# Order of fill pieces, turning waits and output copies in the attention stage of a one-core hybrid block

## The reference, cut to what matters

```python
z = jnp.einsum('bhqd,bhkd->bhqk', qb, kb) * scale
log_keep = jnp.where(valid, jax.nn.log_sigmoid(-z), 0.0)
later = lax.cumsum(log_keep, axis=3, reverse=True) - log_keep
w = jnp.where(valid, jnp.exp(jax.nn.log_sigmoid(z) + later), 0.0)
outs.append(jnp.einsum('bhqk,bhkd->bhqd', w, vb))
```

## Time and profile before

| what | us |
|---|---|
| three runs | 1004.69, 1006.06, 1008.02 (median 1006.06) |
| the profiled execution | 1006.47 |
| span of the profiled execution | 1004.6 |
| PE busy in the span | 960.1 (96%) |
| DVE, ACT, POOL busy in the span | 526.6, 321.1, 193.8 |
| attention stage, 195 to 347 us | 152.0, of it PE busy 138.65, DVE 111.48, ACT 102.50 |
| from the barrier on, 347 us to the end | 657.6 |

### The profile page before, as it was taken

The page is one execution under the profiler, slowest core; times in us unless marked ns, Lnnn a source line. Parts: engine busy times, 40 slices in busy tenths (PEclk is TensorE's granted clock), DMA queues, the critical chain, the costliest instruction groups (busy, mean ns, idle before and its releaser), DMA issues.

```text
span 1004.6 us, 14136 instructions
## 1 busy us (share of the span) xinstructions
PE 960.1 (96%) x5731; PEld 805.3 (80%) x5731; DVE 526.6 (52%) x763; ACT 321.1 (32%) x732; POOL 193.8 (19%) x96
## 2 busy tenths in 40 slices
PE   4999999899999899999999999999999989999998
PEld 3889999677777688888787788888888778788886
DVE  3676895689668254454224338033334466654422
ACT  6552111467776431211451111123322552110000
POOL 0001120160001022112211212100011016873000
PEclk9799999999999999999999999999999999999999
DMA  9860600611210211211222253511212674436231
GB/s 320 225 177 23 189 2 22 202 49 29 59 43 17 58 43 44 62 42 42 63 74 95 95 126 124 140 43 56 61 54 65 237 243 168 129 123 210 86 103 63
DMA packets 120587, 100.58 MB, mean 100 GB/s; under 512 B 18023, under 2 KB 100544, under 8 KB 120266
## 3 DMA queue, kind: packets, MB, share of 16 engines
q1 hardware_dynamic: 90218, 76.07, 25.0%
q10 hardware_dynamic: 30304, 23.60, 7.9%
HBM read 73.44 MB, written 24.12 MB: 97 GB/s over the span
## 4 chain that ended last, share of the span: by engine, by line
PE 90%; DVE 4%; ACT 2%; issue 2%; DMA 1%; SPq 0%; POOL 0%; ACTq 0%; DVEq 0%
PE psum L758 47%; PE psum L266 8%; PE psum L267 7%; PE psum L268 7%; PE psum L1000 3%; PE psum L985 2%; DVE stick L1095 2%; PE psum L971 2%; PE psum L1322 1%; PE psum L973 1%; PE psum L381 1%; PE psum L370 1%; PE psum L1416 1%; PE psum L1422 1%; PE psum L1398 1%
## 5 line engine op out<-in xcount | busy, mean ns | idle before, releaser
L758 PE MATMUL psum<-hhi,w3hl 128*128 128x512 f32 x1120 | 370.8, 401 | 5.4 <-issue 2.7
L758 PEld LDWEIGHTS psum<-hhi,w3hl 128*128 128x128 f32 x1120 | 211.9, 189 | 51.5 <-issue 6.0
L758 PE MATMUL psum<-hlo,w3hl 128*128 128x512 f32 x560 | 219.4, 392 | 0.0
L747 POOL TENSOR_TENSOR w3hl<-w3raw,w3hl 128x1024 fp32r<-128x1024 f32 x43 | 104.7, 2434 | 514.9 <-DVE w3hl L740 514.9
L758 PEld LDWEIGHTS psum<-hlo,w3hl 128*128 128x128 f32 x560 | 106.0, 189 | 21.8 <-issue 1.9
L1095 DVE TENSOR_TENSOR_SCAN stick<-stick,floor 128x1024 f32<-128x1024 f32 (+7 forms) x64 | 94.3, 1511 | 25.4 <-ACT stick L1045 25.3
L266 PE MATMUL psum<-w1hi,hhi 128*128 128x256 f32 (+2 forms) x320 | 99.2, 310 | 0.0
L267 PE MATMUL psum<-w1lo,hhi 128*128 128x256 f32 (+2 forms) x320 | 98.3, 307 | 0.0
L268 PE MATMUL psum<-w1hi,hlo 128*128 128x256 f32 (+2 forms) x320 | 98.1, 307 | 0.0
L758 PE MATMUL psum<-ohi,w3hl 128*128 128x512 f32 x256 | 79.6, 390 | 2.9 <-issue 2.9
L740 DVE CAST w3hl<-w3raw 128x1024 fp32r<-128x1024 f32 x43 | 34.3, 797 | 72.5 <-DMA w3raw<-in_w_in 44.0
(11 more groups left out here) (221 smaller groups left out, 1432.6 us busy)
## 6 DMA issues: line engine op xcount, KB each, us to landing
z_scratch<-zst ACTq DMA_DIRECT2D x44, 256.0 KB, 2.1
w3raw<-in_w_in ACTq DMA_DIRECT2D x20, 512.0 KB, 4.2
ada<-in_ada_w SPq DMA_DIRECT2D x16, 512.0 KB, 6.0
w3raw<-in_w_in SPq DMA_DIRECT2D x16, 512.0 KB, 4.0
sg<-z_scratch SPq DMA_DIRECT2D x8, 1024.0 KB, 4.8
xrow<-in_x SPq DMA_DIRECT2D x4, 1024.0 KB, 6.2
w1raw<-in_w_in SPq DMA_DIRECT2D x4, 1024.0 KB, 7.8
adag<-in_ada_w SPq DMA_DIRECT2D x8, 512.0 KB, 4.3
```

The source lines that it names most:

```text
L747: nc.gpsimd.tensor_tensor(lo, w3raw[:], cast(hi), ALU.subtract).then_inc(w3_lo, 1)
L758: t = nc.tensor.matmul(out_, a[:, kt, :], moving[b][:, kt, 512 * half:512 * half + 512], start=(ends[0] and kt == k0 and m == 0), stop=(en ...
```

## The change

Three edits, all in the attention:

1. In PE's loop `fill_2(pe, n)` moves from behind `flips(n - 1)` to directly behind `scores(n + 2)`, ahead of a turn and of the flips. The pieces and their steps stay.
2. `turn(u)` waits for `fl_ok` at u - 1 in all cases, where for u % 4 of 0 and 1 it waited for u. It thus waits for `low(u - 2)`, the last reader of its bank, and not for `low(u - 1)`. For u = 4, 8 and 12 both values were reached long before, so the edit changes the waits of u = 5, 9 and 13: steps 9, 25 and 41.
3. In ACT's loop `copy_out(m)` of blocks with `qb` < 4 moves from the start of step 2m + 5 to the start of step 2m + 4, ahead of `keep(2m + 6)` and `copy_w(2m + 3)`. Blocks with `qb` >= 4 stay where they are. SP's program, which issues the stores, stays.

```diff
@@ turn(u)
                 if u >= 4:
-                    pe.wait_ge(fl_ok, u - 1 if u % 4 >= 2 else u)
+                    pe.wait_ge(fl_ok, u - 1)
@@ pe_2
                 if n + 2 < NST:
                     scores(n + 2)
+                fill_2(pe, n)
                 if turn_at(n) is not None:
                     turn(turn_at(n))
                 if 1 <= n <= NST:
                     flips(n - 1)
-                fill_2(pe, n)
@@ act_2
             for n in range(NST + 6):
-                if n >= 5 and n % 2 and (n - 5) // 2 < NST // 2:
-                    copy_out((n - 5) // 2)
+                m = (n - 4) // 2
+                if n >= 5 and n % 2 and m < NST // 2 and steps[2 * m][1] >= 4:
+                    copy_out(m)
+                if n >= 4 and n % 2 == 0 and m < NST // 2 and steps[2 * m][1] < 4:
+                    copy_out(m)
```

## The result

The changed kernel takes 1000.19 us (median of 5 runs, 998.05 to 1000.93), the kernel before 1006.06 (5 runs, 1004.69 to 1008.02): ratio 0.9939, 95% interval 0.9925 to 0.9952. The direction was right, the size too small: 1002.1 was forecast, and the result stands at the low end of the range, 1000.0, or by the ratio just outside it (0.9939 x 1006.06 = 999.9).

What follows compares the result with a forecast made beforehand. PE was taken to set the attention stage's pace, busy 138.65 of 152.0 us. Turns 2.56, step 44 -0.32, two output copies 0.27 each and the end 1.17 summed to 3.95 us: 1002.1 us against 1006.06, range 1000.0 to 1005.0.

Steps and rivals of the forecast that it cites:

- turns of pairs 0, 1, 2: Steps 9, 25 and 41: PE's 1.01 us wait before the turn goes, winning 0.85, 0.70 and 1.01 us.
- output copy, step 13: Pair 0, step 12: ACT works off three turns, so swapping the output copy and `copy_w` wins nothing.
- output copies, steps 15 and 31: Output copy goes into ACT's idle time in steps 14 and 30, so PE goes on 0.27 us sooner each time.
- flips late in step 44: The fill piece delays step 44's flips by 0.69 us and `copy_w` with them; PE loses 0.32 us.
- end: End of the attention stage, edits 1 and 3 together: three PE waits shrink, winning 1.17 us (low 0.5, high 1.5).
- the price of the turning wait: At the turns of steps 9, 25 and 41: 1.01 us idle each as the most winnable; 2.56 us forecast together.
- ACT runs without a break: Pair 0, from the `keep` at 226.81 to the output copy PE awaits at 229.45: pair 0 wins 0.85 us.
- nothing there shows as a wait: Flips behind the turn in step 9 need an older running product and copy; no wait was expected there.
- ACT as the bound: Rival: turn casts queue behind ACT's copies, each turn wins only 0.31 us; 1003.7 us, chance 0.23.
- Output copies without effect: Rival: `copy_w`, now second, ends as late, so 3 x 0.27 us fall away; 1002.9 us, chance 0.07.
- The slower case: Rival: flips delayed 0.69 us by each of 16 pieces set the pace; 1012.8 us, chance 0.06.
- The clock: Rival: less idle time before the barrier keeps PE's clock up behind it, 1.6 us more won; 1000.5 us, chance 0.14.

Runs made afterwards that it cites:

- after: The changed kernel with all three edits, against the kernel before, and its profile: 1000.19 us, ratio 0.9939; the profiled execution took 1000.31 us.
- before: The kernel before the change, and its profile: 1006.06 us (median of 5 runs).
- copies_only: Edit 3 alone (output copies of short blocks a step sooner) on the kernel before: 1002.9 us, ratio 0.9972.
- fill_only: Edit 1 alone (fill pieces directly behind the scores) on the kernel before: 1006.58 us, ratio 1.0009.
- turns_only: Edit 2 alone (the turn waits for the low part two back) on the kernel before: 1002.73 us, ratio 0.9965.
- same_again: The kernel before, word for word, run as if it were a change: 1006.79 us, ratio 1.0002.
- all_again: The changed kernel with all three edits, word for word, run once more against the kernel before: 1001.23 us, ratio 0.9955.
- all_third: The changed kernel with all three edits, run a third time against the kernel before: 999.41 us, ratio 0.9944.

## Why the prediction came out as it did

**The sum, term by term.** The gain of 5.01 in the stretch against the 3.95 forecast, in us:

| term | forecast | after | from |
|---|---|---|---|
| turns of pairs 0, 1, 2 | 0.85 + 0.70 + 1.01 | 1.19 + 0.86 + 1.24 | steps 10, 21 to 28, 40 to 42 |
| output copy, step 13 | 0 | 0.20 | steps 10 to 14 |
| output copies, steps 15 and 31 | 0.27 + 0.27 | 0.38 + 0.32 | steps 16, 32 |
| flips late in step 44 | -0.32 | -0.24 | steps 42 to 46 |
| DVE behind step 16 | not seen | -0.43 | steps 16 to 21 |
| end | 1.17 | 1.43 | step 61 to the barrier |
| rest | 0 | 0.06 | |
| sum | 3.95 | 5.01 | |

**The step that failed is the price of the turning wait**, at 2.56 the largest term; with 3.29 in its place it gives 0.73 of the missing 1.06, and it lies above the high end that was set for it, 3 x 1.01 = 3.0. Two of its parts were wrong. First, 1.01 us of idle time was taken for all that PE loses. In before the last scores matmul starts at 222.88 and the turn at 224.22, 1.34 us later. In after:

```profile
220.68 0.34 PE L973 MATMUL psum<-qk 128*128 128x384 f32 x1
220.86 0.60 PE L954 MATMUL psum<-ident,rows 128*128 128x128 f32 x4
...
221.47 0.50 ACT L1045 ACTIVATE stick<-psum 128x384 f32<-128x384 f32 x1
221.84 1.17 ACT L1038 CAST qk<-psum 64x512 fp32r<-64x512 f32 x2
223.04 0.59 ACT L1053 COPY rows<-psum 128x512 f32<-128x512 f32 x1
223.52 0.39 ACT L1045 ACTIVATE stick<-psum 128x256 f32<-128x256 f32 x1
```

0.18 from start to start. A PE matmul starts before the length of the one before it is over, so a wait costs 1.34 - 0.18 = 1.16 where the idle time shown is 1.01. The curve says 1.18 to 1.24, three times. The Trainium skill ("Perfetto Trace Analysis", "Summary: the profiler window per engine type") has it that TensorE's end in a profile is estimated; the trace agrees in so far as the next row begins 0.16 inside the 0.34.

Second, ACT was taken for full where it was not. ACT too starts its next instruction ahead of the end of the last (221.47 + 0.50 = 221.97, next at 221.84), so a row of them lasts less than the sum of their lengths, and short idle times don't show. "ACT runs without a break" was a reading of rows that leave out such gaps. With the shift of 2.20 between the two profiles taken off, `high` came 224.91 - 221.84 - 2.20 = 0.87 sooner where 0.74 was forecast. The `keep` at 226.81 came 226.81 - 223.52 - 2.20 = 1.09 sooner, where 0.85 was forecast, and `values` 229.45 - 226.06 - 2.20 = 1.19. PE's wait ahead of it stayed 0.23, and didn't grow to 0.4:

```profile
226.06 1.09 PE L1000 MATMUL psum<-rows 128*64 128x128 f32 x16 [0.23 <-ACT ost L1060]
```

In pair 1 the turn gave 1.18 and the piece ahead of it took 0.32, not its whole 0.69 from the turn: 0.86 where 0.70 was forecast. In pair 2, 1.24 for 1.01.

**Copies and pieces.** Steps 15 and 31 are right in place and mechanism, 0.11 and 0.05 too small; in step 13 0.20 was won where nothing was forecast. The loss behind step 44 is there, 0.24, though PE's rows show no wait of 0.3 in step 45; without the other edits it was 0.60.

**The end.** The order of the instructions is the one described, `copy_out(29)` and `copy_w` are ahead of the issue of the fill bank's store. The waits forecast were 0.2, 0.5 and 0.7. In after, ACT and PE near the end:

```profile
335.01 0.37 ACT L1053 COPY rows<-psum 128x256 f32<-128x256 f32 x1 [0.73 <-PE psum L985]
335.28 0.59 ACT L833 COPY rows<-psum 128x512 f32<-128x512 f32 x1
335.44 0.32 PE L1000 MATMUL psum<-wTs,rows 128*64 128x128 f32 x1 [0.35 <-ACT rows L1053]
...
336.36 0.27 ACT L1053 COPY rows<-psum 128x128 f32<-128x128 f32 x1 [0.49 <-PE psum L985]
337.11 0.44 PE L1000 MATMUL psum<-rows 128*64 128x128 f32 x4 [0.75 <-ACT rows L1053]
```

Two waits of PE are left, 0.35 and 0.75 (the first, forecast at 0.2, doesn't show), against 0.51, 1.52 and 0.72. From step 61 to the barrier 9.04 fell to 7.61, 7.94 and 7.85 in three profiles of the change, which differ only behind the last `values`. It was credited to both edits together, wrongly: copies_only has 7.29, and fill_only alone makes it 9.36. The gain is the copies' alone, and edit 1 takes 0.3 back.

**What was not seen.** The loss of 0.43 behind step 16. The prediction followed PE and ACT, and of the flips behind the turn it held that "nothing there shows as a wait". The running products are DVE's, and eight steps on DVE was on the edge: before's weight loads waited 0.2 for it at 238.40 already. Who moves one engine by 1.8 us must ask which other engine was nearly late. Here DVE's chain had 2.14 us of standing still beside POOL's split in it, unseen as long as PE was later.

**The rivals.** ACT as the bound: false (turns_only, 1.19 a turn). Output copies without effect: false (copies_only, 2.07). The slower case: false (fill_only, three places only, 0.50 in all). The clock: the granted clock fell again at the barrier, only a microsecond later than before. Windows of after behind the barrier:

```profile
340.00:341.00 1.00, 1.00 (x5) 0.82 (x5) 0.00 (x0) 0.00 (x0) 0.00 (x0) 1.00 0.22 29
341.00:343.00 2.00, 2.00 (x6) 1.57 (x6) 0.00 (x0) 0.00 (x0) 0.00 (x0) 0.53 0.89 248
...
343.00:346.00 3.00, 3.00 (x11) 2.36 (x10) 1.63 (x4) 0.00 (x0) 0.87 (x1) 0.74 0.22 65
```

PE's clock was granted at 2.4 GHz for the first microsecond, at 1.2 GHz for nearly all of the second window and about half of the third. The 30th matmul behind the barrier starts 8.32 us after it, against 8.04 before: nothing won.

**Outside the stage.** The 1.06 us by which the stage beat its forecast would have made 1001.0 of the 1002.1; that the median came to the edge of the range, 1000.19, is the part outside the stage. The stage's 5.03 us are a ratio of 1 - 5.03 / 1006 = 0.9950, inside the intervals of all three measurements of the change (0.9939, 0.9955, 0.9944). What after's 5.87 us of median has beyond it is not a work of the edits as far as the profiles show: the first scores of the fourteen profiles start anywhere from 191.65 to 194.74, before all changed code. At the front the granted clock differs for equal instructions; before, after:

```profile
20.00:45.00 25.00, 24.40 (x135) 22.85 (x134) 16.00 (x23) 14.09 (x22) 0.00 (x0) 0.73 0.86 238
```

```profile
20.00:45.00 25.00, 24.41 (x145) 22.36 (x144) 16.66 (x23) 15.54 (x26) 0.00 (x0) 0.80 0.96 257
```

(0.80 - 0.73) x 25 = 1.75 of the 2.18 us. The clock stood at 1.2 GHz from about 29.0 to 42.6 us in before and from about 30.5 to 40.5 in after (the expectation of same_again has 32.4 for the start). All fourteen profiles fall into these two groups: six have 0.80 in this window and their first scores at 191.65 to 192.51, eight have 0.73 and 193.79 to 194.74. The changed kernel is in both: after has 0.80, all_again and all_third have 0.73. So this part of after's lead is luck and not the edits. Behind the barrier one wait of 1.16 for a low part of POOL (L266 for L1928, at 911.85) has no counterpart in before; but same_again, the kernel before once more, has one of 0.5, and all_again and all_third have 0.6 and 0.5, so it comes and goes without an edit. From barrier to end the profiles lie between 656.7 and 659.5. Why the clock at the front and this wait differ between executions is open; no run here varied it.

## What to carry to other kernels

Price a wait from start to start of the instructions around it, with and without it, and not by the idle time shown; and measure a stage between two marks that leave out what differs from one execution to the next: from step 9 to the last `values` it repeated here to 0.05 us, in two profiles of before and in three of the change, while the run's time scattered over 5. Where PE moves ahead, look for the engine that was nearly late: PE's weight loads show its waits before its matmuls do. Two engines that stand in each other's way are worth untying even if one of them gets all of the work.

## What the runs showed of the hardware

- DVE's running product and POOL's subtraction don't overlap: 0.41 us became 2.55 beside POOL (2.56 in before), 1.99 became 4.14, and POOL's 2.38 became 4.30 when a long product had begun first. The later one ended behind the other: DVE's products 0.28 and 1.88 us behind POOL's end, POOL 2.18 us behind the end of DVE's product.
- The subtraction of 128 x 1024 takes DVE 1.23 us, and POOL some 2.2, counted from the end of the DVE product that it met.
- The same overlap cost nothing to speak of in before and 0.43 to 0.79 us once PE had moved 1.8 us ahead.
- ACT's and PE's rows overlap: ACT's next instruction starts 0.13 us ahead of the end of the last (221.84 and 221.97), PE's turn 0.16 ahead of the end of the scores.
- In the same code near the front the mean granted clock over 25 us was 0.80 in six profiles and 0.73 in eight, the changed kernel's in both groups; the first scores came at 191.65 to 192.51 us in the first and at 193.79 to 194.74 in the second.
